# Two written-out decoder layers: seams in halves of 512 columns, chunk 0's chain ahead of chunk 1's, first FFN blocks per token chunk

## The reference

```python
for l in range(DEPTH):                       # DEPTH = 2
    mod = c_act @ ada_w[l] + ada_b[l]
    sh_m, sc_m, g_m, sh_f, sc_f, g_f = jnp.split(mod, 6, axis=-1)
    h = modulate(rmsnorm(x, mix_pre_g[l]), sh_m, sc_m)      # h * (1 + sc) + sh
    y = mixer_sublayer(h, w_in[l], ...)      # RG-LRU, retention, latent attention, gates, w_out
    x = x + g_m[:, None, :] * rmsnorm(y, mix_post_g[l])
    h = modulate(rmsnorm(x, ffn_pre_g[l]), sh_f, sc_f)
    y = conv_glu(h, ffn_w_up[l], ffn_conv_w[l], ffn_conv_b[l], ffn_w_down[l])
    x = x + g_f[:, None, :] * rmsnorm(y, ffn_post_g[l])
```

## Time and profile before

| | us |
|---|---|
| timed runs: median | 1131.63 |
| timed runs: lowest, highest of 3 | 1122.67, 1131.72 |
| profiled execution, first to last instruction (span) | 1125.7 |
| TensorE busy | 1012.5 |
| VectorE busy | 839.8 |
| ScalarE busy | 532.5 |
| GpSimd busy | 544.1 |

### The profile page before, as it was taken

How to read it: one execution, slowest core, us unless ns; L and a number is a source line. 1 busy time by engine, 2 the same in 40 slices (tenths; PEclk the granted TensorE clock), 3 DMA queues, 4 the chain that set the end, 5 groups by cost and what they waited for, 6 DMA issues and landing times.

```text
span 1125.7 us, 19024 instructions
## 1 busy us (share of the span) xinstructions
PE 1012.5 (90%) x7006; PEld 932.7 (83%) x7006; DVE 839.8 (75%) x886; ACT 532.5 (47%) x663; POOL 544.1 (48%) x365
## 2 busy tenths in 40 slices
PE   5799899789999699999959989878999969999996
PEld 5789887678897699999947989767899769999995
DVE  5867699867777688788766778986676768666665
ACT  0544556244435654555454355724533465544544
POOL 0475684255665258888881468525466615000000
PEclk9999999899999799999988999989999979999998
DMA  9857636264657267776743763726455725555530
GB/s 301 309 169 225 191 132 225 75 187 151 207 189 240 99 210 256 241 256 218 235 151 104 224 195 116 243 75 185 153 180 187 256 89 185 177 181 186 182 117 37
DMA packets 140454, 206.53 MB, mean 183 GB/s; under 512 B 6289, under 2 KB 113115, under 8 KB 140251
## 3 DMA queue, kind: packets, MB, share of 16 engines
q1 hardware_dynamic: 128000, 161.76, 44.7%
q0 software_dynamic: 11520, 41.95, 10.9%
q10 hardware_dynamic: 859, 1.81, 0.4%
HBM read 204.45 MB, written 1.05 MB: 183 GB/s over the span
## 4 chain that ended last, share of the span: by engine, by line
PE 62%; DVE 23%; issue 6%; ACT 5%; DMA 3%; SPq 1%; DVEq 0%; ACTq 0%
PE banks L1426 55%; DVE w_lo L983 6%; ACT w_hi L540 3%; PE banks L1452 2%; DMA raw<-in_w_in 2%; DMA AB<-in_ada_w 1%; DVE AB L1125 1%; DVE EF L1212 1%; DVE h L1034 1%; PE banks L1477 1%; DVE x L1062 1%; DVE lat L1194 1%; PE banks L1562 1%; PE banks L1462 1%; DVE h_lo L1041 1%
## 5 line engine op out<-in xcount | busy, mean ns | idle before, releaser
L1426 PE MATMUL banks<-h_lo,w_hi 128*128 128x256 f32 x1504 | 439.4, 292 | 28.3 <-DVE w_lo L983 20.4
L1426 PE MATMUL banks<-h_hi,w_lo 128*128 128x256 f32 x1504 | 430.8, 286 | 0.0
L1426 PE MATMUL banks<-h_hi,w_hi 128*128 128x256 f32 x1504 | 430.5, 286 | 0.0
L1426 PEld LDWEIGHTS banks<-h_lo,w_hi 128*128 128x128 f32 x1504 | 294.1, 196 | 34.8 <-DVE w_lo L983 22.9
L983 DVE TENSOR_TENSOR w_lo<-raw,w_hi 128x2048 fp32r<-128x2048 f32 (+1 forms) x87 | 238.0, 2743 | 85.6 <-ACT w_hi L540 85.4
L1426 PEld LDWEIGHTS banks<-h_hi,w_lo 128*128 128x128 f32 x1504 | 294.3, 196 | 1.6 <-issue 1.4
L1426 PEld LDWEIGHTS banks<-h_hi,w_hi 128*128 128x128 f32 x1504 | 294.0, 195 | 0.0
L459 POOL TENSOR_TENSOR adp<-adw,cact 128x1024 f32<-128x1024 f32 x80 | 205.8, 2573 | 32.9 <-DMA adw<-in_ada_w 13.4
L540 ACT ACTIVATE w_hi<-raw 128x2048 fp32r<-128x2048 f32 (+1 forms) x87 | 161.4, 1871 | 40.3 <-PE banks L1426 35.1
L470 POOL TENSOR_TENSOR adacc<-adp 128x256 f32<-128x256 f32 x40 | 44.3, 1108 | 278.3 <-PE banks L1462 275.3
L1384 DVE TENSOR_TENSOR w_lo<-raw,w_hi 128x2048 fp32r<-128x2048 f32 x56 | 132.7, 2370 | 17.5 <-ACT w_hi L868 17.1
(11 more groups left out here) (272 smaller groups left out, 1579.2 us busy)
## 6 DMA issues: line engine op xcount, KB each, us to landing
raw<-in_w_in SPq DMA_DIRECT2D x52, 1024.0 KB, 6.0
raw<-in_ffn_w_up SPq DMA_DIRECT2D x44, 1024.0 KB, 5.2
adw<-in_ada_w POOLq DMA_DIRECT2D x80, 512.0 KB, 4.1
raw<-in_ffn_w_down SPq DMA_DIRECT2D x22, 1024.0 KB, 5.0
raw<-in_w_out SPq DMA_DIRECT2D x8, 1024.0 KB, 7.0
raw<-in_ret_wo SPq DMA_DIRECT2D x4, 1024.0 KB, 5.6
raw<-in_lru_wo SPq DMA_DIRECT2D x4, 1024.0 KB, 5.2
raw<-in_mla_wo SPq DMA_DIRECT2D x4, 1024.0 KB, 5.1
```

The lines of the kernel that those rows point to most:

```text
L1426: ins = MM(ps, lhs, rhs, start=first and n == 0, stop=last and n == 2)
```

## The change

1. The loop over layers is a Python loop on every engine, so each layer's instructions stand for themselves with constants in their waits; `cur` goes and parameters are read from `par[:, l]`.
2. The squares, gatings, residuals, scalings, `h_hi` and `h_lo` of a seam are done in halves of 512 columns, and `y_ps` is raised for each half of y. The sum of the first half, with the epsilon, is the bias of the root over the second.
3. `normalise` moves from VectorE to ScalarE; VectorE keeps the reciprocal (`inverse_rms`).
4. Chunk 0's steps up to `h_lo` come before chunk 1's second half of y on both engines.
5. Splits move: at the seam after an FFN, block 0 of the next layer goes between the last pair's two `conv`s and block 1 in front of `half_end`; at the seam before an FFN, block 41 goes behind chunk 0's `h_hi` and `h_lo`.
6. The first two up blocks are taken per token chunk, with 128 token columns a matmul: block 0 for chunk 0, transposes of chunk 1, block 1 for chunk 0, block 0 for chunk 1, an adaLN part, block 1 for chunk 1.
7. The last layer leaves out the preparation of a next one and the eight adaLN parts that nothing reads; x goes out in four DMAs for two.

```diff
@@ ScalarE, post_square
+                junk = (CD, AB)[c][:].rearrange("p a b -> p (a b)")[:, 512 * half:512 * half + 512]
+                A_(junk, PS[:, 2 * c + half, :], ACT.Square, accum_out=sums[:, 1, c, half:half + 1]).then_inc(p_ss.s, 1)
...
@@ ScalarE, half_end
+                post_square(l, ph, 0, 0)
+                post_square(l, ph, 0, 1)
+                if l == L - 1 and ph == 1:
+                    post_square(l, ph, 1, 0)
+                    post_square(l, ph, 1, 1)
+                    return
                 l2, n2 = (l, 2) if ph == 0 else (l + 1, 0)
-                split_block(l2, first)
-                post_square(l, 2 * ph, 0, ph)
                 mean_square(l2, n2, 0)
-                post_square(l, 2 * ph + 1, 1, ph)
+                post_square(l, ph, 1, 0)
+                normalise(l2, n2, 0)
                 act.wait_ge(mod_ready.s, mod_ready.at(l, ph + 2))
                 modulate(l2, n2, 0)
-                if ph == 1:
-                    h_high(l2, n2, 0)
+                h_high(l2, n2, 0)
                 if ph == 0:
                     split_block(l, first + 1)
+                post_square(l, ph, 1, 1)
...
@@ ScalarE, the FFN's last pair
                 gelu(i)
+                A_(st[:, 14:15], st[:, 12:13], ACT.Sqrt)
+                if l + 1 < L:
+                    split_block(l + 1, 0)
                 conv(i * 2 + 1, 1, i)
+                gate_rows(l, 1, 1, 6)
                 hidden_hi(i, 1)
-                gate_rows(l, 1, 1, 6)
-                A_(st[:, 14:15], st[:, 12:13], ACT.Sqrt)
+                if l + 1 < L:
+                    split_block(l + 1, 1)
                 half_end(l, 1, 0)
...
@@ VectorE, half_end
+                gated(l, ph, 0, 0)
+                gated(l, ph, 0, 1)
+                residual(l, ph, 0)
...
+                inverse_rms(l2, n2, 0)
+                gated(l, ph, 1, 0)
                 dve.wait_ge(mod_ready.s, mod_ready.at(l, ph + 2))
+                modulate(l2, n2, 0)
+                h_low(l2, n2, 0)
                 if ph == 0:
+                    split_block(l, first + 1)
+                gated(l, ph, 1, 1)
+                residual(l, ph, 1)
...
@@ TensorE, up_proj and the start of the FFN
-                def up_proj(n, part, slot, j_done):
+                def up_proj(n, part, slot, j_done, cs=slice(0, T)):
...
-                            ins = mm3(PS[:, 4 + part, T * b:T * b + T],
-                                      (wh[:, k, P * b:P * b + P], wl[:, k, P * b:P * b + P]), h_pair(k), k == 0, k == DK - 1)
-                    ins.then_inc(blk_used.s, 1)
+                            ins = mm3(PS[:, 4 + part, T * b + cs.start:T * b + cs.stop],
+                                      (wh[:, k, P * b:P * b + P], wl[:, k, P * b:P * b + P]), h_pair(k, cs), k == 0, k == DK - 1)
+                    if cs.stop == T:
+                        ins.then_inc(blk_used.s, 1)
...
-                to_features(l, 3, 1)
-                pe.wait_ge(n_lo.s, n_lo.at(l, 4))
-                up_proj(0, 0, SLOT[NM], RING + NM + 1)
-                ada_part(ffn_n, 0)
-                up_proj(1, 1, SLOT[NM + 1], RING + NM + 2)
+                for c in range(TC):
+                    cs = slice(P * c, P * c + P)
+                    pe.wait_ge(n_lo.s, n_lo.at(l, 2 * (2 + c) + 2))
+                    up_proj(0, 0, SLOT[NM], RING + NM + 1, cs)
+                    if c == 0:
+                        to_features(l, 3, 1)
+                    else:
+                        ada_part(ffn_n, 0)
+                    up_proj(1, 1, SLOT[NM + 1], RING + NM + 2, cs)
```

234 lines of the change are left out of this document (125 added, 109 removed).

## The result

Four timed runs of the changed kernel have a median of 1152.89 us (1151.29 to 1154.77), four of the kernel before on the same chip 1131.68: a ratio of 1.021, with a 95% interval of 1.017 to 1.025. It is slower by about 2%, clear of the noise; the forecast was 1133 and no measurable change, and the range, 1117 to 1145, missed it. The profiled execution took 1154.77, its span is 1152.9, 27.2 over that of before.

A forecast was written before the change was run, and what follows sets the result against it. It took TensorE, busy 90% of the 1125.7 us span, as the bound. Terms +8.8 + 3.5 - 4.6 - 3.5 - 3.0 = +1.2 gave a span of 1126.9, forecast as a median of 1133 us, range 1117 to 1145.

The forecast's parts named there:

- p: First two up blocks: price of one 128-column fp32r matmul, taken as 0.113 us at 2.4 GHz.
- rival A: First two up blocks: a narrow matmul is paid by its columns, 0.06 us each; total 1118 us; chance 0.11.
- rival C: First two up blocks: a narrow matmul is paid like one of 512 columns, 0.235 us; total 1179; chance 0.09.
- the end: After the last product: no preparation of a layer that isn't there, and halves; -4.6 us (-4 to -5.5).
- the last down product pushed by the splits: Seam from FFN to mixer: block 0's splits stand ahead, so this product starts at 571.5, not 568.79.
- Block 0 for chunk 0 fills TensorE from 370.2 to about 378.1, its first half at the low clock: Layer 0's seam into the FFN: narrow block 0 ends before chunk 1's transposes at 379.3, leaving some 1 us of pause.
- 144 x 0.113: Seams into the FFN: narrow matmuls after chunk 1's transposes, from 379.3, end at 396.1 against 391.7: +4.4 us a seam.
- starts at 370.2 and not 377.5: Layer 0's seam into the FFN: TensorE's first FFN product comes earlier by not waiting for chunk 1.
- FFN to mixer: Seam into layer 1's mixer: moved splits block ScalarE's queue and delay chunk 0's chain; +3.5 us (-2 to +7).
- rival D: Seam from FFN to mixer: ScalarE's blocked queue, low clock and GpSimd stretches cost +12, not +3.5; total 1142; chance 0.13.
- Unread accumulations: Layer 1's FFN: leaving out eight adaLN groups that nothing reads gives -3.5 us (-2.5 to -3.8).
- Register steps: Layers written out: register steps ahead of waits and the copy to `cur` go, -3 us (0 to -8).

The follow-up runs named there:

- e1: The changed kernel with its first two up blocks whole again (both token chunks, 96 matmuls of 256 columns): 1129.12 us, ratio to before 1.000.
- e16: The changed kernel with discarded 256-column matmuls in TensorE's pauses at the two seams into the FFN: 1123.12 us, ratio to before 0.996.
- e13: The written-out kernel without leftovers, pauses unfilled, plus 192 discarded 128-column matmuls behind chunk 1's transposes at each seam into the FFN: 1191.0 us, 1.053.
- e11: The changed kernel with whole blocks and splits back, chunk 1 ahead of chunk 0's later steps, block 41's split behind both, normalising on VectorE: 1109.71 us, 0.986.
- e2: The kernel before with its layers written out instead of looped over, and nothing else: 1121.72 us, ratio 0.9945.
- e3: The kernel before with layers written out and the last layer's leftovers and eight unread adaLN accumulations gone: 1115.03 us, ratio 0.987.

## Why the prediction was wrong

- The miss is 26.0 us of span (1152.9 for 1126.9); 17.0 of it lie in layer 1's seam and 2.6 in layer 0's.
- The price at the full clock was right: 0.112 for p = 0.113; rival A's 0.06 and rival C's 0.235 were not. So were chunk 0's first product (5.1 for 5.5), the end (-4.8 for -4.6), and the last down product pushed by the splits (582.7, that is 571.7 less the 11.0 us by which this stretch begins later, for 571.5).
- The step that failed is "Block 0 for chunk 0 fills TensorE from 370.2 to about 378.1, its first half at the low clock", with "144 x 0.113" behind it. I let the clock come back as in the earlier trace rows, where the blocks are wide. It took 10.3 us in both layers, wholly at 0.213, for 7.9. So chunk 1's transposes, whose input came 0.7 sooner than forecast (382.4 is 13.4 behind the last output product, for 14.1), ended 2.7 later, and that is layer 0's +7.0 for +4.4. In layer 1 the 144 were at 0.213 too: 144 x 0.1 = 14.4, which with the same +7.0 makes its +21.4. e1 (24 us back with wide blocks), e16 (30 back with a full start) and e13 (the low stretch made again with discarded matmuls) show it from three sides. Why layer 1's stream did not get the clock back where layer 0's did stays open; the forecast had no row of a narrow stream behind a pause.
- What the forecast counted on, that TensorE "starts at 370.2 and not 377.5", was worth little. Since a narrow matmul costs nearly what a wide one costs, chunk 1's blocks after `h_lo` take as long as both chunks' would. What chunk 0 does early takes little off the end; what decides is chunk 1's `h_lo`. I compared chunk 0's start as if it were worth something, and priced the w_lo split and the chunk order ahead of chunk 1 only as far as they led to 379.3. e1 puts them at +4.5 a seam, e11 at +7 against a better order.
- FFN to mixer: the mechanism was right (ScalarE's w_hi of block 1 at 591.03, 580.0 by the same count, for 579.4). The term was +4.9 for +3.5, but its steps were off by more: the mixer's first product came 6.1 later, for 2.2. The two passes stretched beside GpSimd (3.68 for 2.29 and 3.12 for 1.42) have 3.1 of it; they were rival D's cause, if not its +12.
- Unread accumulations: -2.8 (e2 to e3) for -3.5. Register steps: -1.6 at the seam and -6.3 in all (e2), of which what is owed to the steps and what to the clock in layer 1's mixer was not separated; the forecast's -3 (0 to -8) lies within.
- The start (+2.3) and layer 0's mixer (+2.0) were priced at 0. In e1 and e16 the same code gives 94.8 and 94.9 for 96.0, and 269.7 and 273.0 for 273.0. What sets these was not tested.

The range failed since rival C, left outside it, priced the width of a matmul, and none priced the clock that the new stream would be granted.
